# Channel-major products of a hybrid backbone step: the two output tiles take turns in two PSUM banks

## What is computed

```python
h = rmsnorm(x, p['norm1_g']) * (1.0 + sc1) + sh1
pool_u, q, k, v, z, xbc, dt_raw, gate_logits = in_projection(h, p['w_in'])
...                                   # pooling mixer, windowed attention, bidirectional SSD scan
g_pool, g_attn, g_ssd = jnp.split(jax.nn.sigmoid(gate_logits), N_BRANCH, axis=-1)
merged = (g_pool * (pool_out @ p['w_pool_o']) + g_attn * (attn_out @ p['w_attn_o'])
          + g_ssd * (ssd_out @ p['w_ssd_o']))
x = x + g1 * (merged @ p['w_out'])
h = rmsnorm(x, p['norm2_g']) * (1.0 + sc2) + sh2
x = x + g2 * (jnp.square(jax.nn.relu(h @ p['w_mlp1'])) @ p['w_mlp2'])
```

## Time and profile before

| | |
|---|---|
| median of 3 runs | 1519.67 us (1517.85 to 1522.13) |
| profiled execution | 1519.58 us, its span 1517.5 us |
| TensorE busy | 1454.3 us, 96% |
| VectorE busy | 888.5 us, 59% |
| ScalarE busy | 670.6 us, 44% |
| GpSimd busy | 114.7 us, 8% |
| granted TensorE clock, mean | 0.989 of full |

### The profile page before, as it was taken

The page is one execution under the profiler, slowest core; times in us unless marked ns, Lnnn a source line. Parts: engine busy times, 40 slices in busy tenths (PEclk is TensorE's granted clock), DMA queues, the critical chain, the costliest instruction groups (busy, mean ns, idle before and its releaser), DMA issues.

```text
span 1517.5 us, 20946 instructions
## 1 busy us (share of the span) xinstructions
PE 1454.3 (96%) x8335; PEld 1325.5 (87%) x8335; DVE 888.5 (59%) x1455; ACT 670.6 (44%) x1164; POOL 114.7 (8%) x107
## 2 busy tenths in 40 slices
PE   6799998999999999999998999989999999999998
PEld 2799777788899899999977997777889999999997
DVE  1786545765466645454647876557645666555562
ACT  2655553433544524242426565442425454334351
POOL 0002100530001000000010030032300010000000
PEclk9899999999999999999999999999999999999999
DMA  9456662132434655655654442223243443333431
GB/s 331 148 170 220 219 189 80 49 118 84 139 111 141 195 194 172 216 181 183 206 165 144 120 114 77 84 57 97 73 122 112 125 124 122 126 122 125 124 121 42
DMA packets 186086, 210.25 MB, mean 139 GB/s; under 512 B 10702, under 2 KB 154374, under 8 KB 185990
## 3 DMA queue, kind: packets, MB, share of 16 engines
q1 hardware_dynamic: 185990, 208.93, 44.2%
HBM read 204.97 MB, written 3.93 MB: 138 GB/s over the span
## 4 chain that ended last, share of the span: by engine, by line
PE 85%; DVE 8%; ACT 4%; issue 1%; DMA 1%; SPq 0%; ACTq 0%; DVEq 0%
PE bank L642 22%; PE bank L643 21%; PE bank L644 21%; PE bank L656 3%; PE bank L657 2%; PE bank L658 2%; PE bank L674 2%; DVE tb L1530 2%; PE seg_ps L674 1%; DVE wlo L1443 1%; PE y_ps L889 1%; PE y_ps L912 1%; PE seg_ps L776 1%; PE y_ps L792 1%; PE y_ps L701 1%
## 5 line engine op out<-in xcount | busy, mean ns | idle before, releaser
L1443 DVE TENSOR_TENSOR wlo<-raw,whi 128x1024 fp32r<-128x1024 f32 (+1 forms) x288 | 352.9, 1232 | 249.9 <-ACT whi L1045 248.8
L642 PE MATMUL bank<-ahi,whi 128*128 128x384 f32 (+1 forms) x1280 | 443.3, 346 | 0.0
L1045 ACT CAST whi<-raw 128x1024 fp32r<-128x1024 f32 (+1 forms) x288 | 297.0, 1036 | 329.1 <-PE bank L644 173.3
L643 PE MATMUL bank<-alo,whi 128*128 128x384 f32 (+1 forms) x1280 | 433.2, 338 | 0.0
L644 PE MATMUL bank<-ahi,wlo 128*128 128x384 f32 (+1 forms) x1280 | 432.9, 338 | 0.0
L642 PE MATMUL bank<-bhi,whi 128*128 128x384 f32 x768 | 262.3, 342 | 1.5 <-ACT arena_s L1092 1.5
L644 PE MATMUL bank<-bhi,wlo 128*128 128x384 f32 x768 | 259.5, 338 | 0.0
L643 PE MATMUL bank<-blo,whi 128*128 128x384 f32 x768 | 259.4, 338 | 0.0
L642 PEld LDWEIGHTS bank<-ahi,whi 128*128 128x128 f32 x1280 | 241.6, 189 | 15.0 <-issue 13.0
L643 PEld LDWEIGHTS bank<-alo,whi 128*128 128x128 f32 x1280 | 241.5, 189 | 4.1 <-issue 3.6
L644 PEld LDWEIGHTS bank<-ahi,wlo 128*128 128x128 f32 x1280 | 241.4, 189 | 0.0
(11 more groups left out here) (229 smaller groups left out, 1394.7 us busy)
## 6 DMA issues: line engine op xcount, KB each, us to landing
raw<-in_w_mlp_dram SPq DMA_DIRECT2D x128, 512.0 KB, 3.6
raw<-in_w_in_dram SPq DMA_DIRECT2D x104, 512.0 KB, 3.8
raw<-in_w_mod_dram SPq DMA_DIRECT2D x96, 512.0 KB, 6.3
raw<-in_w_ssd_o_dram SPq DMA_DIRECT2D x16, 512.0 KB, 3.4
raw<-in_w_out_dram SPq DMA_DIRECT2D x16, 512.0 KB, 3.5
raw<-in_w_pool_o_dram SPq DMA_DIRECT2D x8, 512.0 KB, 3.6
raw<-in_w_attn_o_dram SPq DMA_DIRECT2D x8, 512.0 KB, 3.5
raw<-in_w_in_dram SPq DMA_DIRECT2D x8, 256.0 KB, 3.3
```

The costliest lines, as they stand in the source:

```text
L642: nc.tensor.matmul(dst, uh[:, k, tm_cols(m)], hi[k0 + k], start=first and k == 0, stop=False)
L643: nc.tensor.matmul(dst, uh[:, k, tm_cols(m)], lo[k0 + k], start=False, stop=False)
L1045: nc.scalar.copy(dst, src).then_inc(hi_ready, 1)
L1443: nc.vector.tensor_tensor(rest, full, top.bitcast(F32), ALU.subtract).then_inc(lo_ready, 1)
```

## The change

The loop over the tiles moves inside the loops over k and over the three products. Both tiles are claimed before the first matmul. Each matmul keeps its operands and its bank; each of the two tiles still steps `gemm_step` by one with its last product. The rest of the file is the same, one line further down.

```diff
-                    for m in range(2):
-                        tile = (l, name, 2 * i + m if first and last else i - i % 2 + m)
-                        dst = (claim(tile) if first else bank[BANKS[tile][0]])[:, 0:cols]
-                        for k in range(4):
-                            nc.tensor.matmul(dst, uh[:, k, tm_cols(m)], hi[k0 + k], start=first and k == 0, stop=False)
-                            nc.tensor.matmul(dst, uh[:, k, tm_cols(m)], lo[k0 + k], start=False, stop=False)
-                            ins = nc.tensor.matmul(dst, ul[:, k, tm_cols(m)], hi[k0 + k], start=False, stop=last and k == 3)
-                        ins.then_inc(gemm_step, 1)
+                    tiles = [(l, name, 2 * i + m if first and last else i - i % 2 + m) for m in range(2)]
+                    dst = [(claim(tile) if first else bank[BANKS[tile][0]])[:, 0:cols] for tile in tiles]
+                    for k in range(4):
+                        for n, (w, x) in enumerate(((uh, hi), (uh, lo), (ul, hi))):
+                            for m in range(2):
+                                ins = nc.tensor.matmul(dst[m], w[:, k, tm_cols(m)], x[k0 + k], start=first and k == 0 and n == 0,
+                                                       stop=last and k == 3 and n == 2)
+                                if k == 3 and n == 2:
+                                    ins.then_inc(gemm_step, 1)
```

## The result

The changed kernel takes 1527.76 us (median of 7 runs, 1525.03 to 1528.37), the kernel before 1521.14 us in the same comparison (7 runs, 1517.85 to 1523.9). The ratio is 1.0042 with a 95% interval of 1.0028 to 1.0055: slower by 6.6 us. The forecast was 1522.5 us, 2.9 us over its base of 1519.6, with a range up to 1529. The time is in the range, and the loss is more than twice the forecast. The prediction gave its largest chance, 0.54, to no measurable change and 0.34 to a slower kernel; the interval lies above 1, so slower it is. The profiled execution took 1528.11 us, its span is 1526.1 us, and the mean granted clock 0.986 (0.989 before). Of all runs in this document one, of the kernel with alternation in first units, took 3650.24 us, a slow run whose cause stays open; it is counted in that kernel's median of 12 (1518.51 us without it) and left out of its ratio, mean clock and fit.

A forecast was written before the change was run, and what follows sets the result against it. TensorE, busy 96% of the span, was taken as the bound, mostly by 6144 `gemm_cm` products. Terms of 0.1 + 0.55 + 0.55 + 0.9 + 0.5 + 0.3 = 2.9 us on 1519.58 gave 1522.5 us, range 1516 to 1529.

The forecast's parts named there:

- Part 1: Start-to-start time of the 6144 `gemm_cm` products: changing bank at every product costs 0 +- 1 ns each, taken as 0.
- Rival A: The products' pitch falls: 1474 us if half of an unexplained 15.7 ns each goes, 1426 us if all; chance 0.12.
- Rival E: The product stream loses its full clock for a tenth of its products: 89 us, 1611 us in all; chance 0.01.
- Part 3: In each unit the first tile is complete 1.94 us later, so both evacuations stand in line behind the unit's end.
- terms (a) to (d): Late first tile: program's end 0.55 us, turn of layers 0.55, `so` to `wo` 0.9, `gsb` to `so` 0.5, scan at `gsa` 0.3.
- Term (f): Elsewhere, as in attention rounds and most of the scan, evacuations already run behind the unit's end: 0.
- Term (e): Eight turns inside the MLP: the 3.93 us pair for the hidden rows fits by 0.2 us; price 0.
- Rival B: The MLP's eight turns miss their time and TensorE waits for hidden rows: 1525.3 or 1529.2 us; chance 0.18.
- Rival C: The convolution stage's chain between ScalarE and VectorE slips: 3.3 us, 1525.8 us in all; chance 0.08.
- Part 2: Second banks claimed 2.12 us earlier, at the unit's start: only the first `xbc` unit waits, 0.1 us.

The follow-up runs named there:

- alternation in first units: Kernel before with the changed order and early claims only in units that begin a pair of tiles and do not finish it: 1518.81 us, ratio 0.9986.
- MLP alone: Changed order in the 128 units of the MLP only, the order of the kernel before in all others: 1522.76 us, ratio 1.0008.
- late step alone: Kernel before, its order and claims kept; only the first tile's step is given at the unit's 23rd matmul instead of its 12th: 1524.39 us, ratio 1.0027.
- selective kernel: Changed order in 172 of 256 units, where no forecast or seen wait hangs on the first tile; the others as in the kernel before: 1517.9 us, ratio 0.9986.

## Why the prediction came out as it did

- **Part 1, the pitch: right.** 570 products in the window where 569 stood, 176.1 ns for 176.2, and the same 1526.7 us with and without alternation. Rival A had no ground: of its 15.7 ns a product 0.1 went. Rival E read a rule on changing banks out of the Trainium skill (same page, section "A second HAM failure mode: psum-queue depth-cycling"). The page ties that loss to short idle times between groups of matmuls; this stream has none, and its clock of 1.00 neither bears the page out nor speaks against it. What the trace does show is that a change of bank at every product alone costs no clock.
- **Part 3, terms (a) to (d): right, and shown by the waits.** Program's end 0.47 us for 0.55; turn of the layers 0.48 for 0.55 (as a wait of 0.57 us for L1068, with the 6.08 us behind it unchanged, where I had put it into the 6.08); `so` to `wo` 0.47 each for 0.45; `gsb` to `so` 0.22 each for 0.25; the scan at `gsa` 0.15 each for 0.15. Sum 2.6 us where 2.8 were forecast. Term (f), nothing elsewhere, missed one place, `gpa` 1 of layer 1, with 0.1 to 0.2 us.
- **Term (e): right.** 3.93 us for the pair, 0.26 us of margin where I gave 0.2. Rival B did not come, in the changed kernel nor with the MLP alone. Rival C did not come either: with the late step alone no unit from the first `xbc` to the last is delayed in layer 0. Its price took 0.55 us a pair where its own text has 0.45, which would have made 2.7 us.
- **Part 2, "No other claim costs anything": wrong.** I lined up the earlier claims with evacuation times of the trace before, and did not move these by part 3. The two parts meet at one place: at the first `pool` unit the bank's tile is completed 11 products later and claimed 12 earlier. 0.8 us there, shown by putting that unit back. The first `xbc` claim cost 0.28 us for 0.1, and 0.24 us more came at the units `pool` 2 and `xbc` 6. So the claims are 1.3 us where the sum had 0.1.
- **The clock: missed.** Rival E asked whether the stream would lose its full clock, and answered from the long window. That answer holds. But the scan's start and the turn of the layers were already places where the clock falls behind idle time, and I gave no term to more or longer idle there. The mean clock is 0.9862 over the 12 runs of the changed kernel and 0.9884 before; by the slope that is 2.1 us (2.5 by the slope of before alone). With most of the idle times filled the distance is 4.5 us, not 6.

The account is then: 2.8 us of waits for the late tile, 1.3 us of claims, 2.1 us of half-clock time, less 0.6 us that the MLPs gave back: together 5.6 of the 6.0 us that the means of the 12 and the 65 runs are apart. Named by the steps of the prediction, the sum's 2.9 us lacked 1.2 us in part 2 and 2.1 us for the clock, which rival E had looked for in the stream alone. That the time still lies under 1529 is luck: this bound was drawn for rival B, which did not come.

Two things stay open. Why the stretches come more often with the late first tile is argued, not shown: it adds small idle times just ahead of places with longer ones, and where a stretch falls shifts between executions. And the cause of the 0.1 ns a product is open. It is small but steady: with alternation in first units the lag falls by 0.86 us over the two MLPs, of which the first `xbc` claim takes 0.28 back, and in the selective kernel by 0.6. So 0.6 of the 1 us that these two are under before at equal clock is in their traces; the rest is within what the fit can tell. The early claims add 2.1 us at equal clock to the late step, of which the traces show 1.3 us; the rest is within what the fit can tell.

## What to carry to other kernels

When a change moves both the moment at which a buffer's content is complete and the moment at which the buffer is claimed, move both in the same table before looking for waits: each alone had twelve products of air here, and together they had none. A steady stream at full clock says nothing about the turns between stages; read the granted clock there, window by window, and count what idle time already costs. Where an engine's idle time cannot be removed, unread products in it may be worth more than a reordering: here 0.38% for 96 extra matmuls.

## What the runs showed of the hardware

An accumulating product into another PSUM bank than the one before costs the same as into the same one, to a tenth of a per cent: 176.1 ns for 384 columns at full clock, and 176.2 ns where twelve in a row go to one bank. The granted clock fell behind idle times of TensorE as short as 1.1 us (before, at 1044 us, behind 0.8 and 1.2 us; changed, at 277 us, behind 1.06), and where it falls differs between executions of one kernel: at 277 us in one profile of the changed kernel, at 306 in the other. A stretch that shows as a mean of 0.83 in 10 us cost some 1.6 us, but for those of which the next wait took up a part. So one profile can differ from the next by that much for no reason in the code. With most idle times filled, the runs also lie closer: the 6 from 1514.9 to 1516.5 us, where the 65 of before spread from 1516.2 to 1524.4.
